# Scoring each key-value group on its own 64 rows, with unpadded keys and the mask written first

## The chip, the cores and the metric

The kernel runs on one core of a Trainium2 chip. The core has TensorE (PE in the profile, its weight loads PEld), VectorE (DVE), ScalarE (ACT), GpSimd (POOL) and SyncE (SP), which issues the DMAs. The metric is the device time of one execution in microseconds. Instructions named L1902 and so on are lines of the kernel before.

## The reference

One launch computes three transformer layers on 512 tokens of width 1024 in f32. The first layer, the only one that the change touches, has three kinds of attention over the same tokens, 8 heads of 64 in each, in 2 key-value groups of 4 heads: over selected blocks of keys, over a window, and over the 128 best keys by an index score (plus a small one over 32 compressed keys).

```python
def masked_softmax(s, mask):
    s = jnp.where(mask, s.astype(jnp.float32), NEG)
    p = jax.nn.softmax(s, axis=-1)
    return jnp.where(mask, p, 0.0)
...
        s = jnp.einsum('bsgrd,bskgd->bgrsk', q, k) * ATTN_SCALE   # one of the branches, in short
        p = masked_softmax(s, mask)
        o = jnp.einsum('bgrsk,bskgd->bsgrd', p, v)
```

With 512 tokens the block selection takes all blocks and the window reaches over all of them, so the first two branches have the causal mask alone. Then two layers follow, each with a gated linear recurrence, a latent attention and a feed-forward part, and a last norm.

## The kernel before

All weights come as one stream of 128x1024 tiles through a ring of seven buffers (RAW). ACT rounds each tile to its high part (WH, L559), GpSimd forms the rest (WL, L469), and `mm3` (L1658) multiplies high and low parts in three matmuls. The order of work on every engine is written out by hand, one program for each engine, with semaphores between them; each use of one of the eight PSUM banks goes through `claim` (L1620), which makes PE wait for the last reader of what stood in that bank eight uses before.

The first layer's attention runs as 96 units (`UNITS1`): 64 for branches 0 and 1 (over pairs j of heads, query tiles qt of 128 tokens and groups g) and 32 for branch 2, ordered by query tile. A unit has one head of one group, 128 queries and n = 128 (qt + 1) keys. In iteration u of the loop at L1870 PE issues the scores of unit u, the transposes of unit u - 3 (`T_LAG`) and the product with V of unit u - 4 (`O_LAG`).

The scores of a unit are a product of queries by keys, L1902, and an identity matmul that adds the mask to the same bank, L1910 (causal, 128 columns) or L1907 (top-k mask, n columns). A query tile (`QNT`, `QDT`) holds, for each j, the 64 dimensions of a group 0 head on partitions 0 to 63 and those of a group 1 head on partitions 64 to 127. The keys (`KT`) stand in six slots, a branch and a group each: one half of the partitions has the group's keys, the other half is zero, so that a product over 128 rows gives the scores of one head. GpSimd clears the halves (L525, L526) and ACT copies the keys there from PSUM (L688, L689). PE waits for both ahead of the loop.

When a unit's scores are there, DVE takes the row maximum (L1317), ACT the exponential with the row sum (L734), PE transposes it in blocks of 128 (L1917), ACT or, for every fourth unit, DVE copies it from PSUM (L567, L1326), PE multiplies it by V (L1927), and DVE scales the result into `MIX` (L1347, L1353). Beside this, DVE does a round of the last query tile's top-k in every third unit up to unit 47 (L1267, L1269), and four times, from units 32, 40, 48 and 56, the compressed branch runs (scores L1877, transposes L1886, product L1895). Eight tiles of a later layer's modulation are scaled by ACT (L716), summed by GpSimd (L485) and multiplied by PE (L1784).

Of the kernel before, what the change touches and what calls it, by code (L numbers as in the profile page):

```python
# [34 lines left out]
ACT = mybir.ActivationFunctionType  # L35
F32 = mybir.dt.float32
# [5 lines left out]
P = 128  # L42
D = 1024
KD = D // P
S = 512
NT = S // P
HEADS = 8
DH = 64
# [167 lines left out]
def program(nc, a, known):  # L216

    note = {}
    with ExitStack() as ctx:
        base = (nc.sbuf_base + 63) // 64 * 64  # L220
        KB = 1024

        def at(name, shape, dt, off):
            return nc.alloc_sbuf_tensor_at(name, shape, dt, offset=base + int(off))
# [18 lines left out]
        identb = small("identb", [P, P], BF16, 2)  # L243
        causal = small("causal", [P, P], BF16, 2)
# [40 lines left out]
        MASKB = w("MASKB", [P, 3, S], BF16, 66.25)  # L285
# [19 lines left out]
        QNT = at("QNT", [P, 4, S], F32, 16 * KB)  # L305
        QDT = at("QDT", [P, 4, S], F32, 24 * KB)


        KT = at("KT", [P, 6, S], F32, 32 * KB)
        PR = w("PR", [P, RING, S], F32, 0)  # L310
        PC = at("PC", [P, 2, 8, NCMP], F32, 44 * KB)
        CST = at("CST", [P, 4, 8], F32, 46 * KB)
# [37 lines left out]
        sem = {name: ctx.enter_context(nc.semaphore(name)) for name in SEMAPHORES}  # L350
# [3 lines left out]
        def mark(name, *key, by=1):  # L354

            count[name] += by
            note[(name,) + key] = count[name]
            return by

        def value(*key):  # L360

            if known and key not in known:
                raise KeyError(key)
            return known.get(key, 1)
# [27 lines left out]
        def bank_of(*key):  # L392

            return bank[known.get(("bank",) + key, 0)]
# [55 lines left out]
        def _(pool):  # L450
# [69 lines left out]
                            [P, 8, 2, NCMP]),  # L520
                        ALU.add).then_inc(sem["ca"], mark("ca", kv, i))
            pass_through(("p1", 6, 3), 0)
            pool.wait_ge(sem["full"], value("full", "p1", 6, NT - 1))
            for i in range(3):
                nc.gpsimd.memset(KT[DH:P, 2 * i, :], 0.0)  # L525
                nc.gpsimd.memset(KT[0:DH, 2 * i + 1, :], 0.0).then_inc(sem["pool_set"], mark("pool_set", 2 + i))  # L526
            pass_through(("o1", 0), 0)
            for qt in range(NT):
                pool.wait_ge(sem["read_dve"], value("read_dve", "o", 1, UNITS1.index((2, 3, 1, qt))))
# [18 lines left out]
        def _(act):  # L548
# [127 lines left out]
            b = bank_of("co", 1)  # L676
            act.wait_ge(sem["pool_set"], value("pool_set", 0))
            for g in range(2):
                for r in range(4):
                    last = nc.scalar.activation(VBLK[32 * r:32 * r + 32, g, DH * r:DH * r + DH],  # L680
                                                b[32 * g:32 * g + 32, 0:DH], ACT.Copy)
# [1 line left out]
            evict_group(5)  # L683
            evict_group(6)
            for i in range(3):
                act.wait_ge(sem["full"], value("full", "tk", i))
                b = bank_of("tk", i)
                nc.scalar.activation(KT[0:DH, 2 * i, :], b[0:DH, :], ACT.Copy)  # L688
                nc.scalar.activation(KT[DH:P, 2 * i + 1, :], b[DH:P, :], ACT.Copy).then_inc(  # L689
                    sem["read_act"], mark("read_act", "tk", i))  # L690
            for i in range(4):
                evict(QNT[:, i, :], "tqn", i)
            act.wait_ge(sem["full"], value("full", "tkc"))
            b = bank_of("tkc")
# [24 lines left out]
            for u in range(len(UNITS1) + T_LAG):  # L719
# [7 lines left out]
                if u < len(UNITS1):  # L727
                    n = (UNITS1[u][3] + 1) * P
# [4 lines left out]
                    b = bank_of("s", 1, u)  # L733
# [3 lines left out]
                qt = cmp_tile(u, CMP_EXP)  # L737
# [4 lines left out]
                qt = cmp_tile(u, CMP_MOVE)  # L742
# [6 lines left out]
            for i in range(KD):  # L749
                act.wait_ge(sem["full"], value("full", "tm", i))  # L750
                b = bank_of("tm", i)
# [7 lines left out]
            for layer in range(LAYERS):  # L759
# [60 lines left out]
                for i in range(3):  # L820
                    act.wait_ge(sem["full"], value("full", "tc2", L, i))
                    b = bank_of("tc2", L, i)
# [4 lines left out]
                b = bank_of("tc2", L, 3)  # L827
# [14 lines left out]
                for u in range(len(UNITS2) + O_LAG):  # L842
                    v = u - T_LAG
                    if 0 <= v < len(UNITS2) and evictor(v) == "read_act":
                        h, qt = UNITS2[v]
# [3 lines left out]
                        b = bank_of("t", 2 + L, v)  # L849
                        n = (qt + 1) * P  # L850
# [4 lines left out]
                    if u < len(UNITS2):  # L855
                        h, qt = UNITS2[u]
                        n = (qt + 1) * P
# [4 lines left out]
                        b = bank_of("s", 2 + L, u)  # L862
# [9 lines left out]
                    if u < len(UNITS2):  # L872
                        h, qt = UNITS2[u]
# [743 lines left out]
        def _(pe):  # L1617
# [34 lines left out]
            def full(ins, *key):  # L1652
                return ins.then_inc(sem["full"], mark("full", *key))
# [182 lines left out]
            for kv in range(2):  # L1836
                pe.wait_ge(sem["read_act"], value("read_act", "hid", kv))
                b = claim("ht", kv)
                for c in range(2):
                    last = nc.tensor.transpose(b[:, 64 * c:64 * c + 64], HID[0:64, kv, c * P:(c + 1) * P],  # L1840
                                               ident[0:64, 0:64])
                full(last, "ht", kv)
            for kv in range(2):
                pe.wait_ge(sem["read_act"], value("read_act", "ht", kv))
                b = claim("co", kv)
                for c in range(2):
                    last = nc.tensor.matmul(b[0:64, 0:DH], HIDT[:, kv, c, :], cw2[:, kv, c, :], start=(c == 0),
                                            stop=(c == 1))
# [16 lines left out]
            pe.wait_ge(sem["read_dve"], value("read_dve", "tqd", 3))  # L1865
            pe.wait_ge(step, value("setup"))
            pe.wait_ge(sem["topk"], value("topk", 2))
            pe.wait_ge(sem["pool_set"], value("pool_set", 4))
            pe.wait_ge(sem["read_act"], value("read_act", "tkc"))
            for u in range(nU + O_LAG):  # L1870
                mods(("att", u))
                qt = cmp_tile(u, 0)
                if qt is not None:
                    for g in range(2):
                        b = claim("cs", qt, g)
                        for j in range(4):
                            last = nc.tensor.matmul(b[:, j * NCMP:(j + 1) * NCMP],  # L1877
                                                    QNT[DH * g:DH * g + DH, j, qt * P:(qt + 1) * P],
                                                    KCT[DH * g:DH * g + DH, :], start=True, stop=True)
                        full(last, "cs", qt, g)  # L1880
                qt = cmp_tile(u, CMP_TURN)
                if qt is not None:
                    pe.wait_ge(sem["cmp_p"], value("cmp_p", qt))
                    b = claim("ct", qt)
                    for g in range(2):
                        last = nc.tensor.transpose(  # L1886
                            b[:, g * P:(g + 1) * P],
                            PC[:, qt % 2, 4 * g:4 * g + 4, :].rearrange("p h c -> p (h c)"), ident[:])
                    full(last, "ct", qt)
                qt = cmp_tile(u, CMP_PV)  # L1890
                if qt is not None:
                    pe.wait_ge(sem["read_act"], value("read_act", "ct", qt))
                    b = claim("cpv", qt)
                    for g in range(2):
                        last = nc.tensor.matmul(b[:, g * 256:(g + 1) * 256], PTC[:, qt % 2, g * P:(g + 1) * P],  # L1895
                                                VBLK[:, g, :], start=True, stop=True)
                    full(last, "cpv", qt)
                if u < nU:
                    br, j, g, qt = UNITS1[u]
                    n = (qt + 1) * P  # L1900
                    b = claim("s", 1, u)
                    nc.tensor.matmul(b[:, 0:n], (QNT if br < 2 else QDT)[:, j, qt * P:(qt + 1) * P],  # L1902
                                     KT[:, 2 * br + g, 0:n], start=True, stop=False)
                    if br == 2 and qt:
                        if qt == 3:
                            pe.wait_ge(sem["topk"], value("topk", 3))
                        last = nc.tensor.matmul(b[:, 0:n], identb[:], MASKB[:, qt - 1, 0:n], start=False,  # L1907
                                                stop=True)
                    else:
                        last = nc.tensor.matmul(b[:, n - P:n], identb[:], causal[:], start=False, stop=True)  # L1910
                    full(last, "s", 1, u)
                v = u - T_LAG
                if 0 <= v < nU:
                    pe.wait_ge(sem["read_act"], value("read_act", "s", 1, v))
                    b = claim("t", 1, v)
                    for kb in range(UNITS1[v][3] + 1):
                        last = nc.tensor.transpose(b[:, kb * P:(kb + 1) * P], PR[:, v % RING, kb * P:(kb + 1) * P],  # L1917
                                                   ident[:])
                    full(last, "t", 1, v)
                v = u - O_LAG  # L1920
                if v >= 0:
                    br, j, g, qt = UNITS1[v]
                    pe.wait_ge(sem[evictor(v)], value(evictor(v), "t", 1, v))
                    b = claim("o", 1, v)
                    for kb in range(qt + 1):
                        c = br * P + g * DH
                        last = nc.tensor.matmul(b[:, 0:DH], PT1[:, v % RING, kb * P:(kb + 1) * P],  # L1927
                                                G[4][:, kb, c:c + DH], start=(kb == 0), stop=(kb == qt))
                    full(last, "o", 1, v)
# [14 lines left out]
            for layer in range(LAYERS):  # L1944
# [9 lines left out]
                for q in range(4):  # L1954
# [6 lines left out]
                    for i in range(4):  # L1961
                        n, which = 2 * q + i // 2, ("lr", "li")[i % 2]
                        pe.wait_ge(sem["xc_lo"], value("xc_lo", L, n))
                        b = claim(which, L, n)
# [14 lines left out]
                for tt in range(NT):  # L1979
                    b = claim("qr", L, tt)  # L1980
                    t = slice(tt * P, (tt + 1) * P)
                    for k in range(2):
                        last = mm3(b[:], (CQH[:, k, t], CQL[:, k, t]), wpair(slot, 512 * k, 512), k == 0, k == 1)
# [233 lines left out]
```

## Time and profile before

| | us |
|---|---|
| median of 3 timed runs (lowest, highest) | 1863.71 (1862.32, 1866.21) |
| the profiled execution, its own time | 1857.34 |
| its span, first to last instruction | 1855.5 |
| PE busy | 1774.3 |
| DVE busy | 973.9 |
| POOL busy | 730.1 |
| ACT busy | 715.0 |

The span is cut into what each engine was busy with. "Busy" is a sum over recorded instructions; the ends of matmuls are modelled, and they overlap. An f32 product stands in the trace as two weight loads and two matmuls. In a row, 64*128 is the part of the array that a matmul uses, rows by columns.

### The profile page before, as it was taken

Reading aid. Unit: us, or ns where it says so; the run is one execution under the profiler, and the core shown is the slowest. Engines: PE = TensorE matmul, PEld = TensorE weight load, DVE = VectorE, ACT = ScalarE, POOL = GpSimd, SP = SyncE. Lnnn points to the kernel's source line nnn. Section 1 sums busy time; section 2 is a strip of 40 time slices with the busy share of each in tenths; the row PEclk is TensorE's granted clock in tenths of the full one; section 3 lists DMA queues with packets and bytes.
Section 4 is the critical chain, followed back from the end, with each engine's and each line's share of the span. In section 5 each row is a group of like instructions: output and inputs, shape, how many; then the busy total and the mean of one; then the engine's idle time right before and its main releaser. Section 6 shows DMA issues by size and latency. Waiting matters only on the chain. (4 is left out here: it accounts for less than half of the span.)

```text
span 1855.5 us, 23527 instructions
## 1 busy us (share of the span) xinstructions
PE 1774.3 (96%) x8439; PEld 1436.7 (77%) x8445; DVE 973.9 (52%) x1707; ACT 715.0 (39%) x1234; POOL 730.1 (39%) x317
## 2 busy tenths in 40 slices
PE   6999999989999999899999999999999999999997
PEld 5877777777887766788888887887866788888886
DVE  6999688583679767633333321669966221101112
ACT  5434555523474642332212222365454232222321
POOL 2434111246445302455455545354511544344442
PEclk8999999999999999999999999999999999999998
DMA  6234010053332204455555532232310223232211
GB/s 229 92 102 137 24 35 24 24 194 124 102 113 91 66 26 145 162 204 182 181 181 198 188 136 91 69 125 80 114 34 23 80 91 103 91 101 97 98 57 46
DMA packets 56345, 197.66 MB, mean 107 GB/s; under 512 B 6961, under 2 KB 7985, under 8 KB 56242
## 3 DMA queue, kind: packets, MB, share of 16 engines
q1 hardware_dynamic: 56242, 196.26, 31.4%
q8 instruction: 68, 1.11, 0.3%
q14 instruction: 35, 0.29, 0.1%
HBM read 194.14 MB, written 2.10 MB: 106 GB/s over the span
## 5 line engine op out<-in xcount | busy, mean ns | idle before, releaser
L469 POOL TENSOR_TENSOR WL<-RAW,WH 128x1024 fp32r<-128x1024 f32 x256 | 652.7, 2555 | 924.9 <-ACT WH L559 654.3
L1660 PE MATMUL bank<-HH,WH 128*128 128x512 f32 x1120 | 439.4, 392 | 12.4 <-POOL WL L469 8.6
L1662 PE MATMUL bank<-HH,WL 128*128 128x512 f32 x1120 | 437.7, 391 | 0.0
L1661 PE MATMUL bank<-HL,WH 128*128 128x512 f32 x1120 | 437.4, 391 | 0.0
L559 ACT ACTIVATE WH<-RAW 128x1024 fp32r<-128x1024 f32 x260 | 271.6, 1052 | 267.0 <-PE bank L1662 221.6
L1660 PEld LDWEIGHTS bank<-HH,WH 128*128 128x128 f32 x1120 | 211.3, 189 | 58.8 <-issue 7.7
L1662 PEld LDWEIGHTS bank<-HH,WL 128*128 128x128 f32 x1120 | 211.3, 189 | 44.3
L1661 PEld LDWEIGHTS bank<-HL,WH 128*128 128x128 f32 x1120 | 211.6, 189 | 43.7
L1593 DVE TENSOR_TENSOR HF<-SILU,bank 128x512 f32<-128x512 f32 x44 | 30.3, 688 | 326.0 <-PE bank L1662 323.0
L1660 PE MATMUL bank<-HDH,WH 128*128 128x512 f32 x352 | 137.2, 390 | 0.0
L1662 PE MATMUL bank<-HDH,WL 128*128 128x512 f32 x352 | 137.0, 389 | 0.0
L1661 PE MATMUL bank<-HDL,WH 128*128 128x512 f32 x352 | 136.9, 389 | 0.0
L1660 PE MATMUL bank<-WH,HH 128*128 128x512 f32 (+2 forms) x288 | 111.9, 389 | 22.8 <-DVE WL L1110 10.6
L1604 DVE SCALAR_TENSOR_TENSOR X<-bank,mod,X 128x512 f32<-128x512 f32 x32 | 24.0, 751 | 199.7 <-PE bank L1662 199.7
L929 DVE SCALAR_TENSOR_TENSOR ACC<-RAW,vec,ACC 128x1024 f32<-128x1024 f32 x77 | 113.5, 1475 | 5.1 <-DMA RAW<-in_stream 0.8
L1661 PE MATMUL bank<-WL,HH 128*128 128x512 f32 (+2 forms) x288 | 110.7, 384 | 0.0
L1662 PE MATMUL bank<-WH,HL 128*128 128x512 f32 (+2 forms) x288 | 110.6, 384 | 0.0
L891 ACT ACTIVATE HDH<-HF 128x512 fp32r<-128x512 f32 x44 | 27.8, 631 | 195.1 <-DVE HF L1593 195.1
L1660 PEld LDWEIGHTS bank<-WH,HH 128*128 128x128 f32 x288 | 55.1, 191 | 33.3 <-DVE WL L1110 10.6
L567 ACT ACTIVATE SILU<-bank 128x512 f32<-128x512 f32 x44 | 26.3, 597 | 139.4 <-PE bank L1662 139.4
L1662 PEld LDWEIGHTS bank<-HDH,WL 128*128 128x128 f32 x352 | 66.1, 188 | 13.8
L1660 PEld LDWEIGHTS bank<-HDH,WH 128*128 128x128 f32 x352 | 66.1, 188 | 13.6
(355 smaller groups left out, 2829.8 us busy)
## 6 DMA issues: line engine op xcount, KB each, us to landing
RAW<-in_stream SPq DMA_DIRECT2D x364, 512.0 KB, 3.4
X<-in_xt SPq DMA_DIRECT2D x4, 512.0 KB, 8.1
out_t<-YA SPq DMA_DIRECT2D x8, 256.0 KB, 2.2
ACC<-in_pos SPq DMA_DIRECT2D x1, 256.0 KB
gains<-in_gains SPq DMA_DIRECT2D x1, 224.0 KB
CS<-in_cs SPq DMA_DIRECT2D x1, 128.0 KB
cw<-in_cw SPq DMA_DIRECT2D x1, 128.0 KB
par<-in_par SPq DMA_DIRECT2D x1, 115.0 KB
```

What stands on the lines that cost most here:

```text
L469: nc.gpsimd.tensor_tensor(lo(k)[:], raw(k)[:], hi(k)[:].bitcast(F32), ALU.subtract).then_inc(sem["passed"], mark("passed", *k))
L559: nc.scalar.activation(hi(k)[:], raw(k)[:], ACT.Copy).then_inc(sem["w_hi"], mark("w_hi", *k))
L567: return nc.scalar.activation(dst, b[0:dst.shape[0], 0:n], func, **kw).then_inc(sem["read_act"], mark("read_act", *key))
L891: nc.scalar.activation(HDH[:, f % FH, :], HF[:, f % 2, :], ACT.Copy).then_inc(sem["hid_hi"], mark("hid_hi", L, f))
L929: ins = V.scalar_tensor_tensor(out=acc, in0=raw(k)[:], scalar=c, in1=acc, op0=ALU.mult, op1=ALU.add)
L1593: V.tensor_tensor(HF[:, f % 2, :], SILU[:, f % 2, :], b[:], ALU.mult).then_inc(sem["hid"], mark("hid", L, f))
L1604: ins = V.scalar_tensor_tensor(out=X[:, n, :], in0=b[:], scalar=mod[:, L, 5 * KD + n:5 * KD + n + 1], in1=X[:, n, :], op0=ALU.mult, op1=AL ...
L1660: nc.tensor.matmul(out, A[0], B[0], start=first, stop=False)
L1661: nc.tensor.matmul(out, A[0], B[1], start=False, stop=False)
L1662: return nc.tensor.matmul(out, A[1], B[0], start=False, stop=last)
```

## The change

The keys of both groups are stored together, as they come out of the transpose: `KT` has three slots, with group 0 on partitions 0 to 63 and group 1 on 64 to 127. The clearing on GpSimd and PE's wait for it are gone; ACT copies each slot once, whole. The product of a unit takes only the 64 partitions of its group, of queries and of keys. And the mask's matmul goes first: it starts the bank, and the product adds to it. The other columns of the bank count as unwritten after the mask's matmul, so the product overwrites them.

```diff
-        KT = at("KT", [P, 6, S], F32, 32 * KB)
+        KT = at("KT", [P, 3, S], F32, 32 * KB)
...
             pass_through(("p1", 6, 3), 0)
-            pool.wait_ge(sem["full"], value("full", "p1", 6, NT - 1))
-            for i in range(3):
-                nc.gpsimd.memset(KT[DH:P, 2 * i, :], 0.0)
-                nc.gpsimd.memset(KT[0:DH, 2 * i + 1, :], 0.0).then_inc(sem["pool_set"], mark("pool_set", 2 + i))
...
             for i in range(3):
-                act.wait_ge(sem["full"], value("full", "tk", i))
-                b = bank_of("tk", i)
-                nc.scalar.activation(KT[0:DH, 2 * i, :], b[0:DH, :], ACT.Copy)
-                nc.scalar.activation(KT[DH:P, 2 * i + 1, :], b[DH:P, :], ACT.Copy).then_inc(
-                    sem["read_act"], mark("read_act", "tk", i))
+                evict(KT[:, i, :], "tk", i)
...
-            pe.wait_ge(sem["pool_set"], value("pool_set", 4))
...
                     b = claim("s", 1, u)
-                    nc.tensor.matmul(b[:, 0:n], (QNT if br < 2 else QDT)[:, j, qt * P:(qt + 1) * P],
-                                     KT[:, 2 * br + g, 0:n], start=True, stop=False)
                     if br == 2 and qt:
                         if qt == 3:
                             pe.wait_ge(sem["topk"], value("topk", 3))
-                        last = nc.tensor.matmul(b[:, 0:n], identb[:], MASKB[:, qt - 1, 0:n], start=False,
-                                                stop=True)
+                        nc.tensor.matmul(b[:, 0:n], identb[:], MASKB[:, qt - 1, 0:n], start=True, stop=False,
+                                         skip_group_check=True)
                     else:
-                        last = nc.tensor.matmul(b[:, n - P:n], identb[:], causal[:], start=False, stop=True)
-                    full(last, "s", 1, u)
+                        nc.tensor.matmul(b[:, n - P:n], identb[:], causal[:], start=True, stop=False,
+                                         skip_group_check=True)
+                    r = slice(DH * g, DH * g + DH)
+                    full(nc.tensor.matmul(b[:, 0:n], (QNT if br < 2 else QDT)[r, j, qt * P:(qt + 1) * P],
+                                          KT[r, br, 0:n], start=False, stop=True, skip_group_check=True), "s", 1, u)
```

## Rows read from the trace of the kernel before

**Rows 1.** The page: busy us (share of the span) xinstructions.
```profile
PE 1774.3 (96%) x8439; PEld 1436.7 (77%) x8445; DVE 973.9 (52%) x1707; ACT 715.0 (39%) x1234; POOL 730.1 (39%) x317
```

**Rows 2.** Busy time by stretch: length, busy us per engine, PE clock, DMA share, GB/s.
```profile
204.87:317.45 112.58, 103.28 (x721) 81.66 (x722) 95.54 (x280) 63.77 (x189) 14.13 (x6) 1.00 0.11 34
317.45:373.20 55.75, 53.99 (x352) 43.60 (x354) 29.71 (x97) 31.75 (x94) 11.72 (x5) 0.94 0.06 20
```

**Rows 3.** Waits of weight loads, 204.8 to 317.4: total us, times, longest.
```profile
PEld bank L1927 <- DVE PT L1326: 2.9, 6, 0.8
PEld bank L1895 <- ACT PTC L567: 2.9, 4, 1.9
PEld bank L1886 <- DVE PC L1390: 2.7, 3, 2.0
PEld bank L1917 <- ACT PR L734: 2.5, 8, 0.8
PEld bank L1927 <- ACT PT L567: 1.5, 3, 0.8
...
PEld bank L1902 <- DVE MIX L1347: 1.2, 1, 1.2
```

**Rows 4.** Waits of weight loads, 317.4 to 374.
```profile
PEld bank L1917 <- ACT PR L734: 3.5, 12, 0.3
...
PEld bank L1784 <- POOL ACC L485: 1.5, 1, 1.5
```

**Rows 5.** Order of time, 254.5 to 255.35: start us, us, engine line op, tiles, shapes, count.
```profile
254.37 0.41 PEld L1927 LDWEIGHTS bank<-G,PT 128*128 128x128 f32 x3
...
254.70 0.30 PEld L1902 LDWEIGHTS bank<-KT,QNT 128*128 128x128 f32 x2
...
254.92 0.10 PEld L1910 LDWEIGHTS bank<-causal,identb 128*128 128x128 bf16 x1
...
255.03 0.42 PEld L1917 LDWEIGHTS bank<-ident,PR 128*128 128x128 f32 x4
```

**Rows 6.** Groups by line and shape: count | busy us, mean ns | idle before.
```profile
L1902 PE MATMUL bank<-KT,QNT 128*128 128x512 f32 x32 | 17.0, 613 | 0.0
...
L1797 PE MATMUL bank<-KIT,QIT 64*128 64x512 f32 x8 | 1.9, 589 | 0.0
```

**Rows 7.** Order of time, 251.70 to 251.96, weight loads into the 64-row shape.
```profile
251.58 0.30 PEld L1927 LDWEIGHTS bank<-G,PT 128*128 128x128 f32 x2
251.95 0.18 PEld L1877 LDWEIGHTS bank<-KCT,QNT 64*128 64x128 f32 x1
```

**Rows 8.** Order of time, 253.19 to 253.45, weight loads out of it.
```profile
253.08 0.30 PEld L1877 LDWEIGHTS bank<-KCT,QNT 64*128 64x128 f32 x2
253.43 0.19 PEld L1902 LDWEIGHTS bank<-KT,QNT 128*128 128x128 f32 x1
```

**Rows 9.** Order of time, 86.15 to 86.53.
```profile
85.97 0.39 PE L1661 MATMUL bank<-WL,HH 128*128 128x512 f32 x1
...
86.19 0.39 PE L1662 MATMUL bank<-WH,HL 128*128 128x512 f32 x1
86.51 0.19 PEld L1797 LDWEIGHTS bank<-KIT,QIT 64*128 64x128 f32 x2 [0.35 <-issue]
```

**Rows 10.** Order of time, 190 to 212, what leads up to the first score.
```profile
198.68 0.58 ACT L688 ACTIVATE KT<-bank 64x512 f32<-64x512 f32 x1
...
201.90 2.48 DVE L1308 COPY QDT<-bank 128x512 f32<-128x512 f32 x4 [10.87 <-PE bank L1739]
...
204.46 0.19 ACT L696 ACTIVATE KCT<-bank 64x32 f32<-64x32 f32 x1
...
204.87 0.30 PEld L1902 LDWEIGHTS bank<-KT,QNT 128*128 128x128 f32 x2 [1.47 <-DVE QDT L1308]
```

**Rows 11.** Busy time by stretch, as rows 2, around the clock's fall.
```profile
109.60:113.10 3.50, 3.50 (x18) 1.47 (x17) 3.26 (x10) 2.79 (x6) 0.00 (x0) 1.00 0.00 0
...
327.45:334.28 6.83, 6.83 (x31) 6.04 (x30) 1.72 (x8) 1.48 (x7) 0.00 (x0) 0.50 0.01 2
```

## The prediction

> **What bounds the kernel now.** I start with the engines' busy shares: TensorE (PE) is busy 96% of the span, the next engine 52% [rows 1]. All edited lines belong to one stage, the first layer's attention, so the next view is the table of busy time over its two stretches, 64 units (branches 0 and 1) and then 32 (branch 2) [rows 2]. PE is busy 103.28 of 112.58 us and 53.99 of 55.75 us, so it idles about 9.3 and 1.8 us. VectorE (DVE) is at 95.54 of 112.58 us in the first stretch: close, but with 17 us to spare. The waits of the weight loads say what stops PE [rows 3, 4]: in the first stretch six rows sum to 2.9 + 2.9 + 2.7 + 2.5 + 1.5 + 1.2 = 13.7 us, none longer than 2.0 us, all for a result of DVE or ScalarE (ACT) that comes a bit late. So the stage is a TensorE stream with small holes: what is added to the stream costs time, except what falls into a hole.
>
> Last I read one unit in order of time, where PE waits for nothing [rows 5]. An f32 product goes as two weight loads and two matmuls. The last P.V load starts at 254.59 (three from 254.37, every 0.11); the two loads of the score product at 254.70 and 254.81; the mask's at 254.92; the transposes' at 255.03. Each load hides behind the matmul before it. From the last P.V load to the transposes' load this unit of 128 keys takes 0.45 us.
>
> **The change, part by part.**
> 1. *Fewer rows in the score product.* The rows give no gain in streaming: the 64-row matmul of the index scores with 512 columns takes 589 ns, the 128-row score matmul 613 ns [rows 6]; a weight load takes 0.18 us for 64 rows and 0.19 for 128 [rows 7, 8]. The matmul count stays 192. I take 0; the 24 ns between those means, on every one of them, bounds it at -4.6 us, and as much the other way.
>
> 2. *The array's shape changes twice in every unit.* Today all matmuls of a unit are 128*128. After the edit the score product is 64*128 between a 128-row mask and 128-row transposes. The trace has this change of shape already, around the compressed scores (L1877), four times in each direction. Going in: P.V loads at 251.58 and 251.69, then the first 64-row load at 251.95: 0.26 instead of 0.11 us [rows 7]. Coming out: loads at 253.08 and 253.20, then 128-row at 253.43: 0.23 instead of 0.11 [rows 8]. The other three places read alike. Before the index scores two 512-column matmuls start at 85.97 and 86.19, 0.22 apart, and the 64-row load at 86.51, 0.32 behind [rows 9]. So I read: a load of another shape starts only about 0.10 us after the stream of the last matmul has ended, and then is bare itself, 0.11 us, where it was hidden. No wait is named at L1877, and only "issue" at the index scores.
>  The Trainium skill, "TensorEngine Tiling (Array Packing)", section Tiling Modes, says that a change of the tiling mode, not merely of the tile, drains the engine. By that rule the change is dearer, not cheaper; the page has no figure for it, the trace agrees with its 0.26 and 0.23 against 0.11 us.
>  Now the new unit of 128 keys, from the last P.V load as 0: mask load 0.11; the mask streams when the P.V product is through, 0.16 to 0.22; shape change, score load at 0.32; second score matmul 0.21 us behind its load (as the mask's load, which starts with that matmul, stands 0.22 behind the score load in [rows 5]), so 0.53, streaming to 0.64; shape change, 0.09, transposes' load at 0.73. Against 0.45 that is +0.29 us. Longer units stream more columns in both orders alike, so the difference stays. 96 x 0.29 = 27.8 us of PE work, 18.6 in the first stretch and 9.3 in the second.
>
> 3. *Mask before product.* The count of instructions is the same, and the order is in the sum above. Its cost besides: the bank is "full" about 0.14 us later in the unit (0.64 against 0.50), so the row maximum on DVE, the exponential on ACT and the transpose three units on start that much later. The bank is still claimed once. In branch 2 the wait for the last top-k mask now stands ahead of the score product, with transposes and P.V queued behind it; that mask is made at unit 47 and first used at unit 88, so 0.
>
> 4. *What the holes swallow.* A hole closes if PE reaches the waiting instruction later anyhow. Transposes wait for an exponential three units old: 3 x 0.29 - 0.14 = 0.7 us of grace; the P.V product for a PSUM copy one to two units old, 0.3 to 0.6; the compressed P.V (L1895) for a copy two units old, 0.6; its transposes (L1886) for DVE work four units old, 1.2. Of [rows 3] I leave: L1927 on DVE 0.8 of 2.9 (6 waits); L1895 1.3 of 2.9 (the one of 1.9); L1886 0.8 of 2.7 (the one of 2.0); L1927 on ACT 0.3 of 1.5; the bank wait of L1902 0.4 of 1.2; nothing of L1917's 2.5. That is 3.6 left and 10.1 swallowed. Second stretch [rows 4]: 1.2 of the 1.5 us on GpSimd (four units old) and 1.5 of the 3.5 in twelve short ones, of which some lie under a running matmul: 2.7. Together 12.8 us. Bounds: nothing swallowed, or everything, 13.7 + 1.5 + 3.5 = 18.7. I take 12.8, because DVE, with 95.5 us of work in what becomes 120 us, doesn't take PE's place.
>
> 5. *Keys stored once.* Six ACT copies of 64x512 at 0.58 us [rows 10] become three of 128x512. Each instruction works on all its rows at once, so I give them 0.58 too, and ACT is done 1.7 us earlier. What is late next is DVE's copies of the second queries: they run without a gap from 201.90 to 204.38. The first score load starts 0.22 us after ACT's last key copy (204.65 to 204.87); after the edit it starts as much behind DVE's end, 204.6: -0.3 us. Bounds 0 and -1.7.
>
> 6. *Six GpSimd memsets and their wait go.* The first score load was held by DVE's and ACT's copies, not by them [rows 10], and GpSimd's next work, the weight splits for the output projection, is wanted only after the attention: 0.
>
> 7. *The clock.* The granted clock is at its higher level (2.4 GHz) through the stage but for 327.45 to 334.28, at 0.50 [rows 11]; shortly before, PE had waited 1.5 us for GpSimd's sum, in its shortest units [rows 4]. With more small gaps it could fall more often; with that hole closed it could stay up. The 3.50 us with the index scores, nearly all of it 64-row matmuls, ran at 1.00 [rows 11]. I take 0, with bounds of -3.4 (half of 6.83 us, given back) and +3.4 for each further stretch of that length.
>
> **Sum**: 27.8 - 12.8 - 0.3 = +14.7 us: +8 in the first stretch, +7 in the second. Nothing behind the attention changes; it starts later by this much. The profiled execution took 1857.34 us (span 1855.5); one of its kind would take 1872.0 (span 1870.2). The median of the three timed runs, 1863.71, is 6.4 us above it, so the forecast is 1863.7 + 14.7 = 1878.4 us.
>
> **The rivals.**
> *B, paid in full.* The holes move instead of closing, since the score result is 0.14 us later in each unit and DVE's bursts (a top-k round every third unit) stand where they did: 27.8 - 0.3 = +27.5, 1891.2 us. For it: DVE's 85% share. Against: the grace of three units is six times that delay. 0.10.
> *C, no gap: not slower.* The 0.26 and 0.23 us could be semaphore waits of those instructions (bank claims) and not the array's shape. Then the load of the score product hides behind mask and P.V as today, the unit takes 0.44 to 0.45 us, and the start's 0.3 is left: 1863.4 us. It decides from where the excess is under 0.04 us a unit (3.7 us over 96). Against it: the same distance at four places in different surroundings, and 0.10 us behind a 512-column matmul too. 0.08.
>  The skill's "TensorE: Matmul & The Clock Gate", section Part 3, lets a weight load be pulled ahead of running matmuls if its rows don't conflict or it goes to the spare buffer; that rule alone would give C. The trace disagrees where the shape changes.
> *D, the clock.* It falls in about six more stretches of [rows 11]'s length: 14.7 + 6 x 3.4 = +35, 1899 us. For it: less streaming per microsecond. Against: it held through every hole of up to 2.0 us in the first stretch. 0.05.
> *A, the forecast:* 0.77.
>
> **How the numbers follow.** A alone, with the swallowed part between 9 and 18.7 us and the clock giving back up to 3.4, spans +5 to +18.5, 1869 to 1882. I reach up to B: 1868 to 1890 leaves out C, D and half of B, 0.18. Within 0.2% is 3.7 us, about what a measurement of this kernel can tell. Same: most of C, 0.06; faster, C with the clock's 3.4 or item 1's 4.6 us on top, 0.03; slower 0.91.
>
> **What would show it.** In the changed profile: score rows as 64*128 with counts unchanged; the score load about 0.15 us or more behind the mask's matmul start and the transposes' load 0.20 us (128 keys) behind the second score matmul's; the 64 units in about 120.5 us and the 32 in about 62; waits of L1917 and L1927 for ACT and DVE mostly gone; first score load near 204.6. Wrong would be: score loads at a pace of 0.11 us behind the mask (C), waits as before at a longer stage (B), more than one stretch at clock 0.5 in it (D).

## The result and the profile after

The changed kernel takes 2005.51 us (2001.73 to 2006.88, 4 runs) against 1863.49 us before: a ratio of 1.0757, 95% interval 1.0738 to 1.0776. It is slower by 142 us, far outside the range that I gave. The profiled execution took 2001.73 us, its span is 1999.9.

The page of the changed kernel: busy time, and TensorE's granted clock in 40 slices, in tenths of 2.4 GHz (before it read 8999 and then nines).
```profile
PE 1930.9 (97%) x8439; PEld 1519.5 (76%) x8445; DVE 979.0 (49%) x1707; ACT 714.3 (36%) x1231; POOL 728.3 (36%) x311
...
PEclk8999555555799999999999999999999999999998
```
PE's busy time grew by 157 us with the same 8439 matmuls. Seven slices stand at 5 or 7, and they are the attention. The table by stretch (length, busy us of PE, PEld, DVE, ACT, POOL, clock, DMA share, GB/s), as [rows 2]:
```profile
206.41:407.77 201.36, 201.36 (x723) 134.83 (x722) 98.76 (x284) 64.31 (x189) 14.09 (x6) 0.54 0.06 19
407.77:525.24 117.47, 113.97 (x389) 75.69 (x390) 32.42 (x99) 33.10 (x96) 14.01 (x6) 0.53 0.03 10
```
The 64 units of branches 0 and 1 went from 112.6 to 201.4 us at clock 0.54. The second stretch here reaches to the first transpose of `MIX`; counted so, the attention was 175.7 us long before (204.87 to 380.58) and is 318.8 us long now: +143.1 of the span's +144.4 us. All else takes 1681.1 us, 1679.8 before. The clock's own stretches, as [rows 11]:
```profile
206.41:208.45 2.04, 2.04 (x11) 1.27 (x10) 0.74 (x3) 1.46 (x2) 0.00 (x0) 1.00 0.00 0
208.45:321.09 112.64, 112.64 (x376) 74.41 (x376) 54.04 (x156) 35.87 (x109) 7.04 (x3) 0.50 0.05 19
321.09:327.92 6.83, 6.83 (x46) 4.91 (x47) 5.21 (x15) 2.39 (x6) 0.00 (x0) 1.00 0.00 0
327.92:375.70 47.78, 47.78 (x167) 33.21 (x167) 22.80 (x69) 14.58 (x45) 4.71 (x2) 0.50 0.07 23
375.70:382.53 6.83, 6.83 (x47) 4.74 (x45) 3.81 (x11) 2.10 (x6) 0.00 (x0) 1.00 0.00 0
382.53:519.06 136.53, 135.81 (x443) 88.81 (x444) 42.97 (x126) 40.41 (x118) 14.01 (x6) 0.50 0.04 12
```
The clock falls 2.0 us behind the first score load and stays at 1.2 GHz for 112.64 + 47.78 + 136.53 = 296.95 of the 312.65 us listed. Before, it was down for 6.83 us in this stage. That is one execution; in e4, e13 and e14 below, whose attention is the unchanged one, it was down for 13.65, 15.29 and 13.65 us, and the attention took 178.24, 177.48 and 178.29 us.

The start of the attention, loads of PE, as [rows 10]:
```profile
206.25 0.10 PEld L1899 LDWEIGHTS bank<-causal,identb 128*128 128x128 bf16 x1 [1.57 <-DVE QDT L1300]
206.41 0.29 PEld L1902 LDWEIGHTS bank<-KT,QNT 64*128 64x128 f32 x2
```
The products are 64*128 now. DVE's last query copies are the late ones, as forecast. I expected the waits of the transposes (L1917, now L1909) and of P.V (L1927, now L1919) to be mostly gone. Those of P.V are; the one for ACT's exponential grew from 2.5 to 7.1 us. For results of other engines these are left inside the 64 units (total us, times, longest; compare [rows 3]):
```profile
PEld bank L1909 <- ACT PR L726: 7.1, 10, 1.1
PEld bank L1909 <- ACT PTC L563: 4.3, 4, 1.1
```
They are waits of weight loads alone; by the profile PE itself is busy in all of the 201.36 us, because it is now the slow side.

### The profile page after: what moved, and what is told of

Its sections match the earlier page's. It is cut to its first block and busy times, and to the rows that moved or that the text cites. A ratio compares the mean times of both kernels' runs of the same rounds, so it can differ in the third digit from the quotient of the medians.

```text
span 1999.9 us, 23525 instructions
## 1 busy us (share of the span) xinstructions
PE 1930.9 (97%) x8439; PEld 1519.5 (76%) x8445; DVE 979.0 (49%) x1707; ACT 714.3 (36%) x1231; POOL 728.3 (36%) x311
## 5 line engine op out<-in xcount | busy, mean ns | idle before, releaser
L1652 PE MATMUL bank<-WH,HH 128*128 128x512 f32 (+2 forms) x288 | 113.4, 394 | 20.8 <-DVE WL L1102 10.2
L1309 DVE TENSOR_REDUCE nmax<-bank 128x1 f32<-128x128 f32 (+3 forms) x96 | 47.1, 491 | 142.6 <-PE bank L1902 142.4
L1919 PEld LDWEIGHTS bank<-G,PT 128*128 128x128 f32 x480 | 109.9, 321 | 0.1
L1919 PE MATMUL bank<-G,PT 128*128 128x64 f32 x480 | 107.1, 385 | 0.0
L1909 PEld LDWEIGHTS bank<-ident,PR 128*128 128x128 f32 x240 | 39.5, 204 | 78.6 <-issue 66.1
L485 POOL TENSOR_TENSOR ACC<-ACC,ADA_T 128x1024 f32<-128x1024 f32 x7 | 16.4, 2347 | 223.9 <-POOLq L474 223.9
```

Of the source, the lines that this page charges most:

```text
L1309: V.tensor_reduce(nmax[:, u % 8:u % 8 + 1], b[:, 0:n], AX_X, ALU.max, negate=True).then_inc(sem["nmax"], mark("nmax", 1, u))
L1652: nc.tensor.matmul(out, A[0], B[0], start=first, stop=False)
```

## The experiments

My theory after the result, **ROWS**: a product on 64 of the array's 128 rows counts as less activity to the clock gate, though it gives it as long a stream. Its rivals: **GAPS** (the holes of the shape changes thin the stream), **ORDER** (mask first) and, later, **PAUSE** (a pause brings the clock down, 64-row work keeps it from coming back). Half-clock times below are read from each run's trace, between the first score load and the first transpose of `MIX`.

**e1_order.** The kernel before with the new order alone:
```diff
-  matmul(b[:, 0:n], Q[:, j, tile], KT[:, 2 * br + g, 0:n], start=True, stop=False)
-  last = matmul(mask columns, identb, mask, start=False, stop=True)
+  matmul(mask columns, identb, mask, start=True, stop=False)
+  last = matmul(b[:, 0:n], Q[:, j, tile], KT[:, 2 * br + g, 0:n], start=False, stop=True)
```


> The order alone: the mask's matmul starts the bank and the score product adds to it, but keys stay padded and the product stays 128 rows. No change of shape in a unit. Theory ROWS (the granted clock falls because the score product uses 64 of the array's 128 rows) and theory GAPS (it falls because the two changes of shape per unit put holes into the stream) both expect no effect: 1863 us within 4, clock 1.00 in the attention but for one or two short falls. Theory ORDER (mask first, result later, is what brings it down) expects most of the 142 us: over 1950 us.


Measured: 1863.2 us against 1862.5, ratio 1.0003 (0.9989 to 1.0017), with 14 us at half clock, as in the unchanged attentions of e4, e13 and e14. ORDER falls.

**e2_rows.** The changed kernel with the product first again:
```diff
-  matmul(mask, start=True); matmul(b, Q[r], KT[r, br], start=False, stop=True)
+  matmul(b, Q[r], KT[r, br], start=True); matmul(mask, start=False, stop=True)
```


> The rows alone: keys stored once, product on 64 rows, but product first and mask second as before. Two changes of shape per unit as in the changed kernel. ROWS and GAPS both expect about 2005 us within 10, the clock at 0.50 through nearly all of the attention. ORDER expects 1863 to 1890 us.


Measured: 1985.8 us (1977.7, 1994.0), ratio 1.0663; clock down for 240 us. The time is below the 1995 us that I had expected at least, but far above ORDER's 1890: the fall comes with either order, as soon as rows and shape changes are there. e3 and e4 take these two apart. That it is 20 us below the changed kernel goes with 57 us less at half clock; why the clock came back more often is open.

**e3_switch.** The kernel before with two shape changes in each unit:
```diff
+  matmul(b[:, 0:1], identb[0:DH, :], causal[0:DH, 0:1], start=True, stop=True)
   matmul(b[:, 0:n], Q[:, j, tile], KT[:, 2 * br + g, 0:n], start=True, stop=False)
```


> The changes of shape alone: the kernel before with one matmul added ahead of each unit's score product, 64 rows, 128x1 bf16 (its one column is overwritten by the product that starts the bank again). Every product keeps 128 rows, but each unit changes shape twice. ROWS expects the clock to hold at 1.00 and the time to show the bare price of two changes: about 0.30 us a unit, 29 us of TensorE work, of which the waits swallow some 13: 1880 us (1872 to 1892). GAPS expects the clock at 0.50 through most of the attention: over 1980 us.


Measured: 1876.4 us, ratio 1.0077 (1.0050 to 1.0105), +13.9 us. Its 64 and 31 of its 32 units:
```profile
207.01:327.91 120.90, 117.66 (x786) 90.74 (x785) 96.16 (x281) 64.65 (x189) 14.15 (x6) 0.99 0.09 32
327.91:388.46 60.55, 59.52 (x363) 47.31 (x365) 27.99 (x91) 30.67 (x92) 11.71 (x5) 0.92 0.05 18
```
The clock holds nearly throughout: it is down for 13.65 us of the attention, no more than in the unchanged ones. GAPS falls, and 120.90 us is what I had forecast for the 64 units of the change (120.5). One of the falls stands where the changed kernel's begins, 1.7 us behind the first score load (208.75); here the clock is back after 3.41 us.

**e4_dense64.** The kernel before, eight `gb` tiles of the second part's layer 0 with half of their contraction:
```diff
-  square_tile("gb", n)
+  for k in range(KD): mm3(b, (w_hi[0:DH], w_lo[0:DH]), (HH[0:DH, k], HL[0:DH, k]), ...)   # layer 0 only
```


> The rows without the gaps: in the kernel before, the eight gb tiles of layer 0 of the second part multiply only the upper 64 of every 128 rows (half of the contraction is left out of these eight tiles), 192 matmuls of 512 columns back to back, one change of shape at either end. ROWS expects the clock to fall to 0.50 a few us into this stretch and stay there, 44 us becoming up to 87: 1890 to 1907 us. GAPS expects clock 1.00 and 1863 us within 4.


Measured: 1884.5 us (1881.3, 1887.7), ratio 1.0119. Less than I expected, since the clock didn't fall at once:
```profile
572.37:592.71 20.34, 17.30 (x76) 13.78 (x76) 19.93 (x23) 8.66 (x12) 4.55 (x3) 1.00 0.16 52
592.71:642.40 49.69, 49.69 (x119) 37.88 (x117) 20.92 (x17) 8.55 (x12) 18.57 (x9) 0.50 0.25 85
```
It held for 20 us of 64-row matmuls and fell at 592.71, just behind a wait of PE of 3.04 us for GpSimd (to 592.04). The kernel before has that wait too (3.30 us, to 585.49) and a fall behind it, at 586.87, but of 3.41 us; here it lasted 54.6 us, until 4.4 us behind the last 64-row tile (642.93 to 647.32). This is where PAUSE comes from.

**e5_pair.** The changed kernel by pairs of units:
```diff
-  for u: mask(u); product(u) on rows of g; T(u-3); PV(u-4)
+  for u, u+1: mask(u); mask(u+1); product(u) on rows 0:64; product(u+1) on rows 64:128;
+              T(u-3); PV(u-4); T(u-2); PV(u-3)
```


> The changed kernel with the two groups' units taken in pairs: both masks, then the two 64-row products one behind the other, on different halves of the array, then transposes and P.V of two units as before. ROWS expects the two products to run beside each other, so that both halves of the array work, and the clock to hold at 1.00 but for a few short falls. TensorE work against the kernel before: two changes of shape in a pair instead of none, +0.29 to 0.34 us, and one product hidden, 0.21 to 0.85 us (mean 0.53): about -0.2 us a pair, -10 us over 48, of which new waits (less grace for the exponential, VectorE at 85%) may take half or all: 1852 to 1866 us. If the clock falls for the gaps or for the 64-row form as such, whatever the other half does: over 1930 us.


Measured: 1883.0 us, ratio 1.0115 (1.0094 to 1.0137). 122 us better than the changed kernel, and still a miss: 85 us at half clock (297 there). The pair's four product matmuls do run beside each other:
```profile
254.36 0.80 PE L1905 MATMUL bank<-KT,QNT 64*128 64x128 f32 x4
```
0.80 us for four against 0.79 us for two at the same half clock in the changed kernel:
```profile
222.13 0.79 PE L1902 MATMUL bank<-KT,QNT 64*128 64x128 f32 x2
```
At full clock four of 512 columns take 1.13 us (e5, at 222.06) and two take 1.12 (changed kernel, at 322.88).

**e6_filler.** The changed kernel with more work:
```diff
   b = claim("s", 1, u)
+  matmul(b[:], identb[:], keep[:], start=True, stop=True)
```


> The changed kernel with more work: ahead of each unit's mask one 128-row bf16 matmul of 512 columns (0.21 us at 2.4 GHz, its result is overwritten by the mask that starts the bank again). Shape changes and 64-row products stay. ROWS expects the clock to be granted more of the time, since more of the stream uses all rows: if it holds throughout, 1863 + 14 (the two changes of shape) + 96 x 0.22 = 1898 us, less where waits swallow some; anything under 1970 counts for it. If the filler doesn't help the clock, it costs 0.21 to 0.43 us in each unit: 2025 to 2045 us.


Measured: 2006.8, 2035.0, 2039.6 and 2044.5 us; the ratio, 1.0856 (1.0791 to 1.0921), is that of the two shorter ones. The trace is of the longest, with the clock at 0.53 in the attention. A miss for ROWS as I had sized it. The shortest, 2006.8, is below what I expected if the filler doesn't help (2025), and its mean granted clock is 0.922 against the changed kernel's 0.912: one filler may help a little in some executions. Whether one is too little or the idea is wrong stayed open until e9.

**e7_pair128.** e5_pair with padded keys and 128-row products:
```diff
-  product(u) on rows of g
+  product(u) on all 128 rows, KT[:, 2 * br + g]
```


> The control for the pairs: the same order of work in pairs, mask first, but padded keys and 128-row products, as before. No change of shape, nothing beside each other. It shows what the pairing costs in waits alone: the clock holds, 1863 to 1872 us under either theory; e5_pair against it is the worth of the two halves.


Measured: 1875.3 us, ratio 1.0073 (1.0048 to 1.0097). 3 us above my range, and the clock did not hold as I had expected:
```profile
205.95:397.07 191.12, 172.99 (x1113) 140.25 (x1113) 128.71 (x382) 96.06 (x285) 28.14 (x12) 0.92 0.08 26
```
It was down for 32 us, without one 64-row score product, in five short falls of 3.4 to 10.2 us and the start of a sixth. Against e4's unchanged attention (178.24 us, 13.65 us down, PE idle for 13.6) pairing costs 13 us: PE's idle time grew by 4.5 us (P.V claims a bank whose scores wait for their exponential, L1932 for ACT 4.6 us), and 18 us more at half clock are worth up to 9. So 128 rows alone do not guarantee the clock, and of e5's 85 us at half clock some 32 are there without any 64-row product.

**e8_pair_shared.** e5_pair with one bank for both P.V results:
```diff
-  b = claim("o", 1, v)                      # each unit
+  if g == 0: bo = claim("o", 1, v + 1)      # P.V into bo[:, 64 g : 64 g + 64]
```


> e5_pair with less waiting: the P.V results of a pair share one bank (columns 0 to 63 and 64 to 127), five banks claimed a pair instead of six, so that P.V doesn't take a bank in which scores still wait for their exponential. In e5_pair those waits are 6.1 us at the P.V loads (in the waits' view, L1924 for ACT). ROWS (clock follows how much of the array works, over time) expects the clock to be at 0.50 for less than e5_pair's 85 us of the attention, since waits thin the stream too: 1850 to 1873 us. If the clock depends on the 64-row form alone, it stays at 85 us or more and the time within 6 us of 1883.


Measured: 1873.0 us, ratio 1.0055 (1.0038 to 1.0071); half clock 77 us. At the upper edge of my range, and 10 us faster than e5_pair. The trace is of the slowest of its four executions (1877.9).

**e9_filler3.** Three fillers in place of one:
```diff
+  for _ in range(3): matmul(b[:], identb[:], keep[:], start=True, stop=True)
```


> The changed kernel with three 128-row bf16 matmuls of 512 columns ahead of each mask, 0.64 us a unit at 2.4 GHz, 1.28 us at 1.2. One of them left the clock at 0.50 (2037 us). ROWS says that one was too little: with three, the 64-row product is a small enough part of the stream, and the clock is granted for most of the attention, 1863 + 14 + 61 = 1938 us if throughout, under 2000 in any case, less than the changed kernel takes with less work. If a 64-row f32 product brings the clock down whatever else runs, the fillers cost 60 to 120 us on top: 2065 to 2130 us.


Measured: 1936.8 us (1928.5 to 1946.4), ratio 1.0418. The attention:
```profile
204.11:453.32 249.21, 246.41 (x1398) 150.82 (x1397) 129.41 (x382) 97.94 (x284) 28.33 (x12) 0.98 0.06 20
```
With 288 more matmuls than the changed kernel this one is 69 us faster, at clock 0.98 and not 0.53, and 2 us from the sum of shape changes and fillers (1938). That the 64-row form holds the clock down whatever else runs is refuted: its share of the stream matters.

**e10_branch2.** The change for branch 2 alone:
```diff
+  r = slice(DH * g, DH * g + DH) if br == 2 else slice(0, P)     # rows of queries and keys
```


> The change in branch 2 alone (units 64 to 95: unpadded keys, 64-row products); units 0 to 63 keep 128-row products, mask first. ROWS expects the fall to be local: clock 1.00 in the first 64 units (113 to 116 us), 0.50 through most of the last 32, whose stretch goes from 63 to 100-118 us: 1900 to 1918 us. Theory START (the clock falls in the pause ahead of the first score and 64-row work only keeps it from coming back) expects it to hold for these too, but for the wait for GpSimd's sum near unit 71: either 1870 us, or from there on 0.50.


Measured: 1912.9 us, ratio 1.0269 (1.0251 to 1.0286).
```profile
206.35:321.45 115.10, 106.18 (x722) 86.05 (x723) 95.94 (x280) 63.87 (x188) 14.12 (x6) 0.97 0.10 33
321.45:435.27 113.82, 110.20 (x392) 72.38 (x390) 32.80 (x103) 33.48 (x97) 14.01 (x6) 0.54 0.03 10
```
The effect is local: 0.97 where products have 128 rows (as in e1, whose first stretch is the same work: 115.04 us at 0.97), 0.54 where they have 64. It fell at 331.53, 10 us into branch 2, near the wait for GpSimd's sum, and came back at 440.76. It is no matter of the first pause (START) alone; PAUSE is still open. The 10 us at full clock also show the bare price of two shape changes with the real 64-row product. Score products of neighbouring units of 128 keys, with one transpose and one P.V block between them, start 0.90 us apart:
```profile
329.06 0.48 PE L1912 MATMUL bank<-KT,QDT 64*128 64x128 f32 x2
...
329.96 0.48 PE L1912 MATMUL bank<-KT,QDT 64*128 64x128 f32 x2
```
The same pair with 128-row products starts 0.61 us apart in e1 (328.79 and 329.40): +0.29 us.

**e11_pair_fill1, e12_pair_fill2.** e8_pair_shared with one or two fillers a pair ahead of the wait for the exponential:
```diff
   b = claim("t", 1, v)
+  if w == u: matmul(b[:], identb[:], keep[:], start=True, stop=True)    # e12: in both units
   wait exp(v); transposes of v
```


> e8_pair_shared with one 128-row bf16 matmul of 512 columns in each pair, put into the bank of the pair's first transposes ahead of the wait for the exponential, where TensorE often waits anyway. e8_pair_shared had the clock at 0.50 for 77 of 192 us of the attention. ROWS expects part of that to come back: if all of it, 1873 - 38 + 50 x 0.22 = 1846 us, less any wait that the filler fills; if half, 1863 to 1866. If the clock doesn't move, 1884 to 1895 us. Faster than the kernel before needs at least two thirds of the half-clock time back.

> The same with the matmul ahead of both units' transposes, two in a pair: 100 x 0.22 = 22 us of work. ROWS expects the clock to hold at 1.00 but for about 15 us: 1873 - 31 + 22 = 1864 us, down to 1852 where half of the added matmuls fall into waits. If the clock doesn't move, 1900 to 1915 us.


Measured: 1873.0 us (1.0048, 1.0036 to 1.0060) and 1876.6 us (1.0067, 1.0054 to 1.0080). Half clock 38 and 24 us instead of 77: the fillers gave back clock and cost about as much. Both miss what I had expected: e11 gave back half of the time at half clock, for which I had said 1863 to 1866, and e12 was to take 1852 to 1864. No version that I tried beats the kernel before.

**e13_ffn64.** Half of the contraction left out of fourteen feed-forward tiles (`fg`, `fu`, f = 2 to 8, layer 0), as in e4_dense64, at a place without a pause:
```diff
-  square_tile(kind, f)
+  half_rows(kind, f) if L == 0 and 2 <= f < 9 else square_tile(kind, f)
```


> In the kernel before, fourteen tiles of the feed-forward part of the second part's layer 0 (f = 2 to 8, gate and up) multiply the upper 64 of every 128 rows (half of the contraction is left out of them): 336 matmuls of 512 columns back to back, 76 us, at a place where TensorE has no pause and the clock stood at 1.00. In e4_dense64 the clock held for 20 us of such matmuls and fell only behind a pause of 3.04 us. PAUSE (a pause or a thin stretch brings the clock down, 64-row work only keeps it from coming back) expects 1.00 throughout and 1863 us within 5. ROWS in its plain form (64-row matmuls bring it down by themselves) expects 0.50 through most of the 76 us: 1900 to 1939 us.


Measured: 1905.0 us (1904.1, 1906.0), ratio 1.0225, +42.5 us.
```profile
803.53:839.94 36.41, 36.41 (x168) 29.66 (x168) 13.61 (x16) 10.95 (x14) 16.74 (x6) 1.00 0.57 202
839.94:918.56 78.62, 78.62 (x186) 60.92 (x185) 12.25 (x13) 10.89 (x14) 22.31 (x8) 0.50 0.30 107
```
PE is busy throughout, one matmul behind the other, and the clock falls after 36.4 us and stays down to the end of the stretch and 10 us longer (to 928.68). In the kernel before the same tiles, with 128 rows, lie in a stretch of 378.8 us (774.6 to 1153.4) at 1.00. No pause is needed for a fall: 64-row matmuls alone do it, with a delay. ROWS in its plain form had expected 1900 to 1939 us, PAUSE 1863.

**e14_ffn_mixed.** The same tiles with 64 rows in every second block (112 shape changes, a quarter of the contraction left out):
```diff
+  r = slice(0, DH) if k in (1, 3, 5, 7) else slice(0, P)
```


> The same fourteen tiles with 64 rows in every second block of the contraction: three matmuls of 128 rows, three of 64 and so on, so a change of shape every 0.68 us, 112 in all (a quarter of the contraction is left out of them). The gaps cost 112 x 0.2 = 22 us at most if the clock holds: 1875 to 1886 us. If gaps and 64-row work together bring it down without any pause, over 1900 us, with 0.50 in the stretch.


Measured: 1933.5 us (1931.8, 1935.2), ratio 1.0378; 1.00 for the first 44.6 us, 0.50 for the other 98.6. A stream in which 64-row and 128-row matmuls take turns falls too, a little later than in e13.

**e15_bridge.** The changed kernel with the pause ahead of the first score filled:
```diff
+  b = claim("warm", "att", 0)
+  for _ in range(11): matmul(b[:], identb[:], keep[:], start=True, stop=True)
   wait for the last query copies
```


> The changed kernel with eleven 128-row bf16 matmuls of 512 columns (2.4 us) in the pause ahead of the first score, so that TensorE goes into the attention without it. PAUSE expects the clock to hold at 1.00 into the units, up to the first wait of a microsecond or more, and at least 20 us of the time to come back: under 1985 us. ROWS in its plain form, or gaps and rows together, expects the fall within some us all the same: 2000 to 2010 us.


Measured: 1960.7 us, ratio 1.0534 (1.0512 to 1.0556), 45 us less than the changed kernel.
```profile
206.47:259.25 52.78, 52.78 (x316) 35.14 (x315) 42.41 (x125) 31.22 (x91) 4.72 (x2) 1.00 0.09 31
259.25:366.12 106.87, 106.87 (x409) 73.57 (x409) 54.69 (x158) 32.57 (x99) 9.39 (x4) 0.56 0.06 20
```
Without the pause the clock holds for 52.8 us, as PAUSE had it, and the time lies in PAUSE's range (under 1985), not in that of plain ROWS (2000 to 2010). But then it falls all the same, with PE busy in all of the 52.78 us, where PAUSE wanted a wait of a microsecond or more. The pause makes the fall come early; it is not its cause.

## Why the prediction was wrong

**The step that failed is item 7, the clock: "I take 0".** It is a term of about +128 us: 142 less the 13.9 of the shape changes (e3) and nothing for the order (e1). Rival D named the outcome, falls of the clock, with six more stretches of 6.83 us, about 41, at a chance of 0.05; it was 297 us. D's reason, less streaming per microsecond, was not the one. Two readings led there. I took 3.50 us of 64-row index scores at 1.00 as a sign that such matmuls are harmless, while the clock can hold for 20 us (e4) or 36 us (e13) of them and fall then: the evidence was too short for a stage of 170 us. And I thought of D as a matter of gaps, which are small, and argued from the holes that the clock had survived. e3 has the gaps without the rows and holds; e13 has the rows without the gaps and falls. Even the argument from the holes rested on one execution: in e4, whose attention is unchanged, the clock fell at 268.44 and 299.17 among the first 64 units, for 3.41 us each. The score product is the largest part of PE's work in the stage (73.6 us of busy time before, P.V 66.0, transposes 42.9), so halving its rows was the large step, and I had booked "fewer rows" at no effect in item 1, where only the duration was looked at.

The Trainium skill, "TensorE: Matmul & The Clock Gate", section Part 1, says that the gate follows how busy PE has been; by that rule alone a stretch with PE busy in all 78.62 of 78.62 us would run at the higher level, and e13's ran at 0.50. The measurement decides: busy time isn't all that counts.

**Item 2, the price of two shape changes**, stood: 0.29 us a unit, as e10 shows with the real product (0.90 against 0.61). With item 4 it gave 27.8 - 12.8 = 15.0 us. e3 is the nearest measurement of that difference, with an added matmul that isn't the change itself: the kernel became 13.9 us longer, and its attention, 191.65 us, 13.4 to 14.2 us longer than those of e4, e13 and e14, which have as much time at half clock. **Item 4's** share isn't settled by it: against e4, PE's busy time in e3's attention grew by 20.0 us and its idle time fell by 6.5, where I had 27.8 and 12.8; busy time has modelled ends, so it need not show the gaps. In the changed kernel the half clock covers this, and one part was wrong there: I had all of L1917's 2.5 us swallowed, and that wait grew to 7.1.

**Item 3, the order:** +0.7 us in e1, inside its interval: 0, as taken. With 64 rows the order seems to matter (e2, 20 us), through the clock, for a reason I have not found.

**Item 5, the start:** the first score load came 2.97 us behind the start of DVE's query copies before (201.90 to 204.87) and 2.70 us after (203.71 to 206.41): -0.27, forecast -0.3. The load stands later than the forecast's 204.6 because DVE's copies start 1.8 us later; ahead of them the trace has a fall of the clock of 3.41 us at 123.12 that the trace of before doesn't have. **Item 6**, the memsets: nothing shows, as taken.

**Item 1** was right for what it said (a 64-row product is no faster: 0.79 us for two matmuls of 128 keys at half clock, 0.78 before at 329.57) and missed what it did to the clock. **Rival C** fell: the gap is there, 0.16 us from mask load to score load where loads of one shape follow every 0.11, and e3 pays for it. **Rival B** can't be told from the changed kernel, where the half clock covers it; e3's +13.9 us is near the forecast's 14.7 and not B's 27.5.

## What to carry to other kernels

On TensorE a product that uses half of the rows costs the same time and can cost the clock: padding with zeros to 128 rows, which looks like waste, kept 2.4 GHz here, and taking it away cost 142 us. Before a long stage is moved to fewer rows, ask what part of its stream then works on the whole array, and don't take a short stretch at full clock as proof; where half products can't be avoided, run two on the two halves at once, though here that still ended 10 us behind the padded kernel (e8). A change of shape has a price of its own, some 0.15 us each (0.29 for two in e10), which small waits partly hide.

## What the runs showed of the hardware that I had not expected

- The clock's level depends on rows in use, not on busy time alone: PE busy for 78.62 of 78.62 us at 0.50 (e13). The padded product had the same nonzero keys and ran at 1.00, so nonzero keys aren't what counts. What share of full-row work keeps the clock up isn't measured here.
- More work can be faster: 288 more matmuls, 69 us less (e9).
- 128-row products can lose the clock too, where waits thin the stream: 32 us at half clock in e7, against 14 to 15 in unchanged attentions. That the waits are the reason is argued, not shown.
- The fall comes late without a pause (36.4 us in e13, 44.6 in e14, 52.8 in e15) and 2.2 us behind one of 1.33 us (changed kernel, 206.25 to 208.45). With 128-row products a fall at that place lasted 3.41 us (e3); with 64-row ones the return mostly waits for the end of the half-row work: 109 us in e10 and 55 us in e4, where the kernel before has 6.83 and 3.41.
- Products on different halves run beside each other: four matmuls in the time of two (e5, 1.13 us and 1.12).
